# Dilated attention in a two-block model: the value projection with activations stationary

## The chip, the cores and the metric

One core of a Trainium2 chip runs the whole program. The metric is the device time of one execution in microseconds; the kernel is one launch of 2.5 ms, and the change touches one stage of it.

## The reference

The reference is a stack of blocks on a sequence of 256 positions with 1024 features (a first model with memory, RWKV and gated mixers, then a second one with HGRN2 and dilated attention), with feed-forward blocks between. What matters here is the second model's dilated attention:

```python
kv = (_rms(x, kv_norm) @ w_kv).reshape(bsz, seq, 2, B_GROUPS, B_HEADS, B_HEAD_DIM)   # 3 groups, 16 heads of 64
k = _rms(kv[:, :, 0], k_gain[:, None, :])
v = kv[:, :, 1]
...
q = _rms((h @ w_q).reshape(bsz, seq, B_GROUPS, B_HEADS, B_HEAD_DIM), q_gain) * (B_HEAD_DIM ** -0.5)
for g, (window, dil) in enumerate(zip((128, 512, 2048), (1, 4, 16))):
    s = einsum(q_g, k_g) + bias_g          # masked to the band of the window, every dil-th key
    p = exp(s - lse); o_g = p @ v_g
o = sum over g of softmax over g (lse)[g] * o_g
return o.reshape(bsz, seq, 1024) @ w_o
```

Since the three groups are weighted by the softmax of their log-sums, the kernel takes one softmax over the keys of all three.

## The kernel before

**Weights.** Every projection streams its weights as slabs of 128 output features by 1024 inputs (512 KB), through a ring of 4 slots (`raw`, `hi`, `lo`). For each slab s, SyncE loads `raw` once the slot's `lo` is made, ScalarE writes `hi` (`act_hi`, L348, rounded to fp32r) once the slot's old `hi` is used, VectorE writes `lo = raw - hi` (`dve_lo`, L356), and TensorE multiplies. A product in full precision is three fp32r matmuls for each of the 8 blocks of 128 inputs: weights high by activations high (L410), weights high by activations low (L414), weights low by activations high (L415). A slab in `pe_slab` is therefore 24 matmuls, each with a 128x128 piece of the weights stationary and 256 columns (the positions) moving; the result has features on partitions and positions in columns. Engines keep their order by counting semaphores: `lo_ready`, `slab_used`, `banks_freed` (a result bank is evicted), and the stage's own counters `d.<name>`.

**The dilated stage** (class `Dilated`) makes the output in 8 rounds c, each a tile of 128 features, that is two heads in three groups. A round has 9 slabs in a hand-written order: first q, k, v in three groups each (the first round k, q, v), i = 0 to 8. The result banks of the slabs turn through banks 0, 1, 2. Between the slabs TensorE does the attention of this round and the one before; after slab i it does:

- i=1: scores of half 0 of the round before (L1785, 12 small matmuls); i=2: the value transposes (`pe_values`, L1754, 6 transposes by the identity, since the values come out with features on partitions and are wanted with positions there)
- i=2, 3, 4: the query square sums (L1765, 4 matmuls of 2 columns each)
- i=4 and 5: transposes of the probabilities, half 1 (12) and half 0 (6) (L1797)
- i=6: the key square sums (L1739, 6 matmuls), then the output of half 1 (L1812, 24); i=7: the output of half 0 (L1812, 12)
- i=8: the scores of half 1 of this round (L1785)

VectorE evicts each slab's bank times the reciprocal norm (L1960 keys, L1962 queries, L1964 values into `dVF`), makes the low half of the slab four ahead, and does the attention's arithmetic in between: `dve_keys`, `dve_bias` (scores, scales and bias added, L2013, then the largest, L2016, and its negative, L2019), `dve_normalize` (L2026, L2030), `dve_heads` (L2036). ScalarE makes the high half, the squares (L1884), the exponentials (L1921), the copies of the transposed probabilities (L1929) and values (L1912, L1913 into `dVT`) and of the output (L1944).

After the eighth round the output projection's slabs (`so`) are interleaved with what is left of round 7's attention: their first 5 input blocks between the scores, the value transposes and the probability transposes, the rest later.

Of the kernel before, what the change touches and what calls it, by code (L numbers as in the profile page):

```python
# [30 lines left out]
P = 128  # L31
T = 256
# [1562 lines left out]
class Dilated:  # L1595


    FIRST, ORDER = (tuple((x, g) for x in order for g in range(GROUPS)) for order in ("kqv", "qkv"))

    def __init__(self, sh, name, nxt):  # L1600
        self.sh, self.k, self.next_gain = sh, sh.k, nxt
        k, a = sh.k, sh.k.A0
        nc = k.nc
        self.base = sh.stage["dil_k0"].base
        self.so = sh.stage["dil_o"]
        self.K = [k.at(f"dK{z}", a + 3 * z * KB, [P, GROUPS, T]) for z in range(2)]
        self.RK = k.at("dRK", a + 6 * KB, [P, GROUPS, T])
        self.KSQ = k.at("dKSQ", a + 9 * KB, [P, GROUPS, T])
        self.Q = [k.at(f"dQ{z}", a + (12 + 3 * z) * KB, [P, GROUPS, T]) for z in range(2)]
        self.QSQ = k.at("dQSQ", a + 18 * KB, [P, GROUPS, T])  # L1610
        self.VF = k.at("dVF", a + 21 * KB, [P, GROUPS, T])
        self.VT = k.at("dVT", a + 24 * KB, [P, 2, GROUPS, P])
        self.S = k.at("dS", a + 27 * KB, [P, 2, 9, P])
        self.st = k.at("dst", a + 37 * KB, [P, 4, 2, 2])
        self.RQ = k.at("dRQ", a + 37 * KB + 64, [P, 2, 2, GROUPS, 2])
        self.GG = k.at("dGG", a + 37 * KB + 192, [P, GROUPS])
        self.RR = k.at("dRR", a + 38 * KB, [P, T])
        self.B = [k.at(f"dB{z}", (86 + 6 * z) * KB, [P, 2, GROUPS, T]) for z in range(2)]
# [18 lines left out]
    def bank(self, s):  # L1637

        return self.k.bank[(s - self.base) % 3]

# [7 lines left out]
    def turned_banks(self, c, half):  # L1648
# [3 lines left out]
        return ((3, 4), (4, 2)) if c < NC - 1 else ((4, 4), (5, 2))  # L1652

    def value_banks(self, c):

        return 6, 3 if c < NC - 1 else 7

# [12 lines left out]
    def pe(self, pe):  # L1670
# [3 lines left out]
        for c in range(NC):  # L1674
            for i, (x, g) in enumerate(self.order(c)):
                s = self.slab(c, x, g)
                if x == "q":
                    sh.pe_slab(pe, s, self.bank(s), lambda kc: (k.Hh[:, kc, :], k.Hl[:, kc, :]),
                               (lambda kc: pe.wait_ge(k.h_lo, n + kc + 1)) if c == g == 0 else None)
                else:  # L1680
                    sh.pe_slab(pe, s, self.bank(s), lambda kc: (k.Kh[:, kc, :], k.Kl[:, kc, :]),
                               (lambda kc: pe.wait_ge(k.kv_lo, kc + 1)) if c == i == 0 else None)
                if c == 0 and i == 0:
# [4 lines left out]
                if c and i == 1:  # L1688
                    self.pe_scores(pe, c - 1, 0)
                if c and i == 2:  # L1690
                    self.pe_values(pe, c - 1)
                if i == (6 if c else 3):
                    self.pe_key_sums(pe, c)
                if i - (2 if c else 4) in range(GROUPS):
                    self.pe_query_sums(pe, c, i - (2 if c else 4))
                if c and i == 4:
                    self.pe_transposes(pe, c - 1, 1)
                if c and i == 5:
                    self.pe_transposes(pe, c - 1, 0)
                if c and i == 6:  # L1700
                    self.pe_output(pe, c - 1, 1)
                if c and i == 7:
                    self.pe_output(pe, c - 1, 0)
# [6 lines left out]
        early, late = range(last - 2), range(last - 2, last - 1)  # L1710
        sh.pe_slab(pe, s, k.bank[0], moving, ready, chunks=early, whole=False)
        self.pe_scores(pe, last, 0)
        for m in range(1, 3):
            sh.pe_slab(pe, s + m, k.bank[m], moving, chunks=early, whole=False)
        self.pe_values(pe, last)
        sh.pe_slab(pe, s + 3, k.bank[3], moving, chunks=early, whole=False, spare=RING)
# [24 lines left out]

    def pe_values(self, pe, c):

        k = self.k
        k.dve_done.wait(pe, f"d.v{c}")
        k.dve_done.wait(pe, f"d.add{c}.1")
        if c == NC - 1:
            k.dve_done.wait(pe, f"d.ol{c - 1}")
        first, rest = (k.bank[b] for b in self.value_banks(c))
        for half in range(2):  # L1750
            for g in range(GROUPS):
                j = GROUPS * half + g
                out = first[:, j * P:(j + 1) * P] if j < 4 else rest[:, (j - 4) * P:(j - 3) * P]
                ins = pe.transpose(out, self.VF[:, g, half * P:(half + 1) * P], k.ident)  # L1754
        k.pe_done.done(ins, f"d.vt{c}")

# [32 lines left out]
    def pe_transposes(self, pe, c, half):  # L1789

        k = self.k
        k.dve_done.wait(pe, f"d.p{c}.{half}")
        k.act_done.wait(pe, f"d.vt{c}" if half else f"d.pt{c}.1")
        places = [(b, j) for b, n in self.turned_banks(c, half) for j in range(n)]
        per_head = len(places) // 2
        for n, (b, j) in enumerate(places):
            ins = pe.transpose(k.bank[b][:, j * P:(j + 1) * P], self.S[:, n // per_head, 3 * half + n % per_head, :], k.ident)  # L1797
        k.pe_done.done(ins, f"d.t{c}.{half}")

    def pe_output(self, pe, c, half):  # L1800

        k = self.k
        k.act_done.wait(pe, f"d.vt{c}")
        k.act_done.wait(pe, f"d.pt{c}.{half}")
# [11 lines left out]
    def act(self, act):  # L1816
# [4 lines left out]
        for c in range(NC):  # L1821
            for i, (x, g) in enumerate(self.order(c)):
                s = self.slab(c, x, g)
                sh.act_hi(act, s + RING, s % RING, 8, s // RING + 1)
                if c == 0 and i == 1:
# [11 lines left out]
                if c and i == 1:  # L1837
                    self.act_exp(act, c - 1, 1)
                if c and i == 2:
                    self.act_values(act, c - 1)  # L1840
                if i - (1 if c else 3) in range(GROUPS):
# [7 lines left out]
                if i == (4 if c else 6):  # L1849
                    self.act_query_scales(act, c)  # L1850
                if i == (5 if c else 2):
# [6 lines left out]
                if c and i == 7:  # L1858
                    self.act_heads(act, c - 1)
        last = NC - 1  # L1860
        self.act_exp(act, last, 1)
        self.act_values(act, last)
        self.act_exp(act, last, 0)
# [41 lines left out]

    def act_values(self, act, c):

        k = self.k
        k.pe_done.wait(act, f"d.vt{c}")
        first, rest = (k.bank[b] for b in self.value_banks(c))  # L1910
        flat = self.VT[:].rearrange("p h g f -> p (h g f)")
        k.act_done.done(act.activation(flat[:, :512], first[:], ACT.Copy), f"d.vt{c}")  # L1912
        k.act_done.done(act.activation(flat[:, 512:], rest[:, :T], ACT.Copy), f"d.vt{c}")  # L1913

# [31 lines left out]
    def dve(self, dve):  # L1946
# [4 lines left out]
        for c in range(NC):  # L1951
            z = c % 2
            for i, (x, g) in enumerate(self.order(c)):
                s = self.slab(c, x, g)
                if c == 0 and x == "q" and g == 0:
                    k.act_done.wait(dve, "d.rr")
                dve.wait_ge(k.slab_used, s + 1)
                bank = self.bank(s)[:, :T]
                if x == "k":
                    ins = dve.tensor_tensor(self.K[z][:, g, :], bank, k.RKV[:], ALU.mult)  # L1960
                elif x == "q":
                    ins = dve.tensor_tensor(self.Q[z][:, g, :], bank[:, ::-1], self.RR[:], ALU.mult)  # L1962
                else:
                    ins = dve.tensor_tensor(self.VF[:, g, :], bank, k.RKV[:], ALU.mult)  # L1964
                ins.then_inc(k.banks_freed, 1)
                if g == GROUPS - 1:
                    dve.wait_ge(k.banks_freed, RING + s + 1)
                    d(dve.engine_nop(), {"k": f"d.kraw{c}", "q": f"d.qraw{c}", "v": f"d.v{c}"}[x])
                if i == (7 if c else 4):
                    self.dve_keys(dve, c)  # L1970
                sh.dve_lo(dve, s + RING, s % RING, 8)
                if c == 0 and i == 1:
# [5 lines left out]
                if c and i == 3:  # L1978
                    self.dve_normalize(dve, c - 1, 0)
                if c and i == 8:  # L1980
                    self.dve_heads(dve, c - 1)
                if i == 8:
                    self.dve_bias(dve, c, 1)
        last = NC - 1
# [1313 lines left out]
```

## Time and profile before

| | |
|---|---|
| three runs | 2557.51, 2553.10, 2557.44 us, median 2557.44 |
| profiled execution | 2556.5 us, its span 2554.7 us |
| busy in the span | TensorE matmuls 97%, VectorE 68%, ScalarE 52%, GpSimd 3% |
| the dilated stage | about 2060 to 2368 us of the span |

The profile is one execution. Times are from the start of the span. PE is TensorE's matmuls, PEld its loads of the stationary operand, which overlap them; DVE is VectorE, ACT ScalarE. In names such as `bank<-Kh,hi` the moving operand stands first and the stationary one second; `Kh` and `Kl` are the activations for keys and values, `Hh` and `Hl` those for queries. Shapes such as `128*128 128x256` are the stationary and the moving operand.

### The profile page before, as it was taken

The numbers are of one execution on the slowest core, as the hardware profiler recorded it, in microseconds if no ns is written. First come the engines' busy times: TensorE is split into PE (matmuls) and PEld (weight loads), VectorE is DVE, ScalarE is ACT, GpSimd is POOL, SyncE is SP. The second block draws the span as 40 slices with busy tenths as digits, with TensorE's granted clock in tenths as the row PEclk, the third lists the DMA queues.
The fourth block names the chain that finished last, engine by engine and source line by source line (L and its number), as shares of the span: only waits on it lengthen the run. The fifth ranks groups of instructions, "written<-read, shape, count | busy, mean of one in ns | idle before, by whom it ended". The sixth has DMA issues, their size and how long they took to land.

```text
span 2554.7 us, 60487 instructions
## 1 busy us (share of the span) xinstructions
PE 2489.3 (97%) x23329; PEld 2423.8 (95%) x23329; DVE 1744.9 (68%) x2871; ACT 1316.9 (52%) x1997; POOL 79.0 (3%) x122
## 2 busy tenths in 40 slices
PE   8998998999999999999999999899999999999999
PEld 8997977989999999989999999899999999999999
DVE  6757677567766757767766767967667666666774
ACT  5534444455545546555545547455455455555552
POOL 0000442000000000000000000000000000000000
PEclk9999999999999999999999999999999999999999
DMA  6663301435655656445655655246656665553664
GB/s 203 218 211 125 100 12 44 149 126 181 208 185 188 212 202 185 153 136 182 207 181 188 211 176 190 75 126 201 203 173 201 200 188 153 157 157 111 195 210 136
DMA packets 119840, 425.14 MB, mean 166 GB/s; under 512 B 16673, under 2 KB 24564, under 8 KB 119412
## 3 DMA queue, kind: packets, MB, share of 16 engines
q1 hardware_dynamic: 111616, 411.65, 49.7%
q10 hardware_dynamic: 8052, 11.04, 2.3%
q8 instruction: 127, 2.08, 0.3%
q14 instruction: 45, 0.37, 0.0%
HBM read 421.51 MB, written 1.12 MB: 165 GB/s over the span
## 4 chain that ended last, share of the span: by engine, by line
PE 87%; DVE 5%; ACT 3%; issue 2%; POOL 1%; SPq 0%; DMA 0%; ACTq 0%; DVEq 0%; POOLq 0%
PE bank L492 20%; PE bank L487 20%; PE bank L491 20%; PE bank L410 5%; PE bank L415 4%; PE bank L414 4%; ACT hi L348 1%; PE bank L2410 1%; DVE lo L356 1%; PE bank L468 1%; PE bank L470 1%; PE bank L469 1%; PE bank L1812 1%; PE bank L1785 1%; PE bank L1797 1%
## 5 line engine op out<-in xcount | busy, mean ns | idle before, releaser
L356 DVE TENSOR_TENSOR lo<-raw,hi 128x1024 fp32r<-128x1024 f32 (+1 forms) x728 | 935.3, 1293 | 381.0 <-ACT hi L348 379.2
L348 ACT ACTIVATE hi<-raw 128x1024 fp32r<-128x1024 f32 (+1 forms) x728 | 782.2, 1106 | 292.9 <-PE bank L415 168.1
L487 PE MATMUL bank<-Hh,hi 128*128 128x256 f32 x3024 | 836.3, 277 | 3.1 <-DVE lo L356 2.0
L492 PE MATMUL bank<-Hh,lo 128*128 128x256 f32 x3024 | 837.4, 277 | 0.0
L491 PE MATMUL bank<-Hl,hi 128*128 128x256 f32 x3004 | 830.1, 276 | 0.0
L487 PEld LDWEIGHTS bank<-Hh,hi 128*128 128x128 f32 x3024 | 567.9, 188 | 4.3 <-DVE lo L356 4.0
L492 PEld LDWEIGHTS bank<-Hh,lo 128*128 128x128 f32 x3024 | 568.1, 188 | 0.0
L491 PEld LDWEIGHTS bank<-Hl,hi 128*128 128x128 f32 x3004 | 564.3, 188 | 0.0
L487 PE MATMUL bank<-Ah,hi 128*128 128x256 f32 x1408 | 389.7, 277 | 1.9 <-DVE lo L356 1.9
L492 PE MATMUL bank<-Ah,lo 128*128 128x256 f32 x1408 | 390.1, 277 | 0.0
L491 PE MATMUL bank<-Al,hi 128*128 128x256 f32 x1400 | 387.2, 277 | 0.0
L487 PEld LDWEIGHTS bank<-Ah,hi 128*128 128x128 f32 x1408 | 265.1, 188 | 2.1 <-DVE lo L356 2.1
L492 PEld LDWEIGHTS bank<-Ah,lo 128*128 128x128 f32 x1408 | 265.1, 188 | 0.0
L491 PEld LDWEIGHTS bank<-Al,hi 128*128 128x128 f32 x1400 | 263.6, 188 | 0.0
L790 ACT ACTIVATE sgate<-gate 128x256 f32<-128x256 f32 x176 | 73.6, 418 | 228.7 <-DVE gate L823 228.7
L795 ACT ACTIVATE Ah<-act 128x256 f32 (+1 forms) x176 | 73.7, 419 | 215.2 <-DVE act L832 215.2
L410 PE MATMUL bank<-Hh,hi 128*128 128x256 f32 x560 | 160.0, 286 | 0.0
L677 DVE SCALAR_TENSOR_TENSOR X<-bank,X 128x256 f32<-128x256 f32 x112 | 47.5, 424 | 163.0 <-PE bank L492 155.1
L415 PE MATMUL bank<-Hh,lo 128*128 128x256 f32 x560 | 155.9, 278 | 0.0
L414 PE MATMUL bank<-Hl,hi 128*128 128x256 f32 x559 | 155.4, 278 | 0.0
L599 ACT ACTIVATE Hh<-X,vec 128x256 fp32r<-128x256 f32 x96 | 47.8, 504 | 196.6 <-DVE X L677 193.8
L410 PE MATMUL bank<-Kh,hi 128*128 128x256 f32 x384 | 111.6, 291 | 0.0
(445 smaller groups left out, 4042.3 us busy)
## 6 DMA issues: line engine op xcount, KB each, us to landing
raw<-in_w SPq DMA_DIRECT2D x600, 512.0 KB, 3.7
raw<-in_w SPq DMA_DIRECT2D x128, 704.0 KB, 4.9
dB<-dil_bias ACTq DMA_DIRECT2D x16, 384.0 KB, 10.4
X<-in_x SPq DMA_DIRECT2D x2, 512.0 KB, 5.9
mem_x<-in_mem ACTq DMA_DIRECT2D x2, 512.0 KB, 4.4
gWS<-in_ws ACTq DMA_DIRECT2D x1, 1024.0 KB
gBS<-in_bs ACTq DMA_DIRECT2D x1, 1024.0 KB
out_x<-X SPq DMA_DIRECT2D x4, 256.0 KB, 2.6
```

The source lines that it names most:

```text
L348: act.activation(k.hi[:, q, :w], k.raw[:, q, :w], ACT.Copy).then_inc(k.hi_ready, 1)
L356: dve.tensor_tensor(k.lo[:, q, :w], k.raw[:, q, :w], k.hi[:, q, :w].bitcast(F32), ALU.subtract).then_inc(k.lo_ready, 1)
L410: pe.matmul(out, wh, xh, start=first and kc == 0, stop=False)
L414: pe.matmul(out, wh, xl, start=False, stop=False)
L415: mm = pe.matmul(out, wl, xh, start=False, stop=last)
L487: pe.matmul(out, wh, xh, start=first, stop=False)
L491: pe.matmul(out, wh, xl, start=False, stop=False)
L492: mm = pe.matmul(out, wl, xh, start=False, stop=last)
L599: eng.activation(k.Hh[:, c, :], src[:, c, :], ACT.Copy, scale=scale).then_inc(k.h_hi, 1)
L677: dve.scalar_tensor_tensor(k.X[:, c, :], k.bank[s % RING][:, :T], coef, k.X[:, c, :], ALU.mult, ALU.add).then_inc(k.banks_freed, st.per_tile)
L790: act.activation(k.sgate[:, j, :], k.gate[:, j, :], ACT.Silu).then_inc(k.silu_done, 1)
L795: act.activation(k.Ah[:, bass.ds(m, 1), :].rearrange("p a t -> p (a t)"), k.act32[:, j, :], ACT.Copy).then_inc(k.ah_ready, 1)
```

## The change

The value slabs swap roles: a half of the activations (128 positions) is stationary, and the weights move. The result has positions on partitions, as the output matmuls want it. Two of the three value slabs, which lie in neighbouring slots, move side by side in one matmul of 256 columns; the third is done alone in 128 columns. The value transposes and VectorE's value evictions go. ScalarE evicts the value banks with a per-position scale, a column `dRC` that two small matmuls and a copy make once in the first round. The single slab is i=6, the pair i=7 and 8 (group order 2, 0, 1). With the pair come changes of order: output of half 0 moves to i=6, `act_heads` and `dve_heads` come before the splits of i=7, `dve_bias` of half 1 before the low split of i=8, bank numbers skip one a round, and the output projection's first slabs start in another order.

```diff
-    FIRST, ORDER = (tuple((x, g) for x in order for g in range(GROUPS)) for order in ("kqv", "qkv"))
+    FIRST, ORDER = (tuple((x, g) for x in order for g in ((2, 0, 1) if x == "v" else range(GROUPS))) for order in ("kqv", "qkv"))
...
-        return self.k.bank[(s - self.base) % 3]
+        c, i = divmod(s - self.base, 9)
+        return self.k.bank[(8 * c + min(i, 7)) % 3]
+
+    def spare(self, c, i):
+
+        return 4 if c and i < 2 else 3
...
+                elif x == "v":
+                    if i < 8:
+                        self.pe_value_slabs(pe, s, 1 if i == 6 else 2)
...
-                if c and i == 2:
-                    self.pe_values(pe, c - 1)
...
+                if c == 0 and i == 4:
+                    for half in range(2):
+                        ins = pe.matmul(k.bank[7][:, 12 + 2 * half:14 + 2 * half], k.RKV[:, half * P:(half + 1) * P],
+                                        k.ident[:, 0:2], start=True, stop=True)
+                    k.pe_done.done(ins, "d.rc")
...
                 if c and i == 6:
                     self.pe_output(pe, c - 1, 1)
-                if c and i == 7:
                     self.pe_output(pe, c - 1, 0)
...
-        sh.pe_slab(pe, s, k.bank[0], moving, ready, chunks=early, whole=False)
+        sh.pe_slab(pe, s + 1, k.bank[1], moving, ready, chunks=early, whole=False, spare=5)
         self.pe_scores(pe, last, 0)
-        for m in range(1, 3):
-            sh.pe_slab(pe, s + m, k.bank[m], moving, chunks=early, whole=False)
-        self.pe_values(pe, last)
+        sh.pe_slab(pe, s + 2, k.bank[2], moving, chunks=early, whole=False, spare=5)
+        sh.pe_slab(pe, s, k.bank[0], moving, chunks=early, whole=False, spare=1)
+        k.dve_done.wait(pe, f"d.add{last}.1")
...
+    def value_columns(self, w, s, n, kc):
+
+        q, cols = s % RING, slice(kc * P, (kc + 1) * P)
+        if n == 1:
+            return w[:, q, cols]
+        return w[:, q:q + 2, cols] if q < RING - 1 else w[:, ::1 - RING, cols]
+
+    def pe_value_slabs(self, pe, s, n):
+
+        k = self.k
+        pe.wait_ge(k.lo_ready, s + n)
+        pe.wait_ge(k.banks_freed, RING + s - 2)
+        for kc in range(NC):
+            wh, wl = (self.value_columns(w, s, n, kc) for w in (k.hi, k.lo))
+            for half in range(2):
+                out = self.bank(s)[:, half * n * P:(half + 1) * n * P]
+                if n == 2:
+                    out = out.rearrange("p (g f) -> p g f", g=2)
+                xh, xl = (x[:, kc, half * P:(half + 1) * P] for x in (k.Kh, k.Kl))
+                pe.matmul(out, xh, wh, start=kc == half == 0, stop=False, skip_group_check=True)
+                pe.matmul(out, xh, wl, start=False, stop=False, skip_group_check=True)
+                ins = pe.matmul(out, xl, wh, start=False, stop=kc == NC - 1, skip_group_check=True)
+        ins.then_inc(k.slab_used, n)
...
@@ ScalarE
+                if c and i == 7:
+                    self.act_heads(act, c - 1)
+                if i == 7:
+                    self.act_values(act, c, 1)
+                    self.act_values(act, c, 2)
                 sh.act_hi(act, s + RING, s % RING, 8, s // RING + 1)
...
+    def act_values(self, act, c, n):
+
+        k, s = self.k, self.base + 9 * c + 5 + n
+        act.wait_ge(k.slab_used, s + n)
+        act.wait_ge(k.banks_freed, RING + s)
+        if c:
+            k.pe_done.wait(act, f"d.o{c - 1}.0")
+        else:
+            k.act_done.wait(act, "d.rc")
+        for half in range(2):
+            out = self.VT[:, half, 2, :] if n == 1 else self.VT[:, half, :2, :].rearrange("p g f -> p (g f)")
+            ins = act.activation(out, self.bank(s)[:, half * n * P:(half + 1) * n * P], ACT.Copy, scale=self.RC[:, half, 0:1])
+            k.act_done.done(ins, f"d.vt{c}.{n}")
+        k.act_done.wait(act, f"d.vt{c}.{n}")
+        act.sem_inc(k.banks_freed, n)
...
@@ VectorE
-                else:
-                    ins = dve.tensor_tensor(self.VF[:, g, :], bank, k.RKV[:], ALU.mult)
...
                 if i == (7 if c else 4):
                     self.dve_keys(dve, c)
+                if c and i == 7:
+                    self.dve_heads(dve, c - 1)
+                if i == 8:
+                    self.dve_bias(dve, c, 1)
                 sh.dve_lo(dve, s + RING, s % RING, 8)
...
-                if c and i == 8:
-                    self.dve_heads(dve, c - 1)
-                if i == 8:
-                    self.dve_bias(dve, c, 1)
```

## Rows read from the trace of the kernel before

**Rows 1.** The page's busy times, shares of the span and instructions.
```profile
PE 2489.3 (97%) x23329; PEld 2423.8 (95%) x23329; DVE 1744.9 (68%) x2871; ACT 1316.9 (52%) x1997; POOL 79.0 (3%) x122
```
**Rows 2.** TensorE's waits, 2060 to 2365 us: total us, times, longest.
```profile
PE bank L410 <- DVE lo L356: 1.4, 1, 1.4
...
PE bank L1739 <- ACT dKSQ L1853: 0.4, 1, 0.4
```
**Rows 3.** Busy times of one round; columns PE, PEld, DVE, ACT, POOL, PEclk, DMA, GB/s.
```profile
2141.00:2176.60 35.60, 35.60 (x320) 33.88 (x319) 24.70 (x45) 19.85 (x34) 0.00 (x0) 1.00 0.57 156
```
**Rows 4.** TensorE in order of time, second half of a round: start, us, what.
```profile
2144.29 0.37 PE L410 MATMUL bank<-Kh,hi 128*128 128x256 f32 x1
...
2147.12 1.46 PE L1739 MATMUL bank<-dKSQ,masks 128*128 128x256 f32 x6
2148.50 1.53 PE L1812 MATMUL bank<-dPT,dVT 128*64 128x128 f32 x24
2149.96 0.39 PE L410 MATMUL bank<-Kh,hi 128*128 128x256 f32 x1
...
2152.99 0.88 PE L1812 MATMUL bank<-dPT,dVT 128*64 128x128 f32 x12
2153.79 0.38 PE L410 MATMUL bank<-Kh,hi 128*128 128x256 f32 x1
...
2156.81 1.57 PE L1785 MATMUL bank<-dK,dQ 64*128 64x256 f32 x12
2158.31 0.38 PE L410 MATMUL bank<-Hh,hi 128*128 128x256 f32 x1
```
**Rows 5.** TensorE in order of time, at the value transposes.
```profile
2167.68 0.82 PE L1754 MATMUL bank<-masks,dVF 128*128 128x128 f32 x6
2168.34 0.51 PE L1765 MATMUL bank<-sel,dQSQ 128*128 128x2 f32 x4
```
**Rows 6.** Timeline at the first query sum, and at a split slab matmul elsewhere.
```profile
2072.53 0.54 PEld L1765 LDWEIGHTS bank<-sel,dQSQ 128*128 128x128 f32 x4
2072.65 0.50 PE L1765 MATMUL bank<-sel,dQSQ 128*128 128x2 f32 x4
...
2072.98 0.19 PEld L410 LDWEIGHTS bank<-Hh,hi 128*128 128x128 f32 x1
...
46.22 0.30 PEld L396 LDWEIGHTS bank<-Hl,hi 128*128 128x128 f32 x2
46.33 0.30 PE L396 MATMUL bank<-Hl,hi 128*128 128x192 f32 x2
...
46.67 0.28 PE L487 MATMUL bank<-Hh,hi 128*128 128x256 f32 x1
```
**Rows 7.** VectorE in order of time, after a round's end and in the tail.
```profile
2158.07 1.23 DVE L356 TENSOR_TENSOR lo<-raw,hi 128x1024 fp32r<-128x1024 f32 x1 [0.72 <-ACT hi L348]
...
2159.55 2.44 DVE L2013 SCALAR_TENSOR_TENSOR dS<-bank,dRQ,dB 128x256 f32<-128x256 f32 x6
...
2163.88 0.42 DVE L1962 TENSOR_TENSOR dQ<-bank,dRR 128x256 f32<-128x256 f32 x1
...
2171.34 1.15 DVE L2030 TENSOR_SCALAR dS<-dS,dst 128x768 f32<-128x768 f32 x2
...
2344.91 1.15 DVE L2030 TENSOR_SCALAR dS<-dS,dst 128x768 f32<-128x768 f32 x2
```
**Rows 8.** ScalarE in order of time, after a round's end.
```profile
2156.98 1.06 ACT L348 ACTIVATE hi<-raw 128x1024 fp32r<-128x1024 f32 x1 [2.50 <-PE bank L415]
```
**Rows 9.** TensorE in order of time, the wide probabilities' transposes, round and tail.
```profile
2175.16 0.31 PE L1797 MATMUL bank<-masks,dS 128*128 128x128 f32 x1
...
2346.44 0.38 PE L1797 MATMUL bank<-masks,dS 128*128 128x128 f32 x2
```
**Rows 10.** The slab loads (L391) of the stage, from issue to landing.
```profile
DMA to landing us min/median/max: 3.2/4.3/10.8
```

More of the change, by code:

```diff
@@ L1610, in __init__ @@
         self.QSQ = k.at("dQSQ", a + 18 * KB, [P, GROUPS, T])
-        self.VF = k.at("dVF", a + 21 * KB, [P, GROUPS, T])
         self.VT = k.at("dVT", a + 24 * KB, [P, 2, GROUPS, P])
@@ L1617, in __init__ @@
         self.RR = k.at("dRR", a + 38 * KB, [P, T])
+        self.RC = k.at("dRC", a + 39 * KB, [P, 2, 2])
         self.B = [k.at(f"dB{z}", (86 + 6 * z) * KB, [P, 2, GROUPS, T]) for z in range(2)]
@@ L1652, in turned_banks @@
         return ((3, 4), (4, 2)) if c < NC - 1 else ((4, 4), (5, 2))
-    def value_banks(self, c):
-        return 6, 3 if c < NC - 1 else 7
     def block(self, half, e, j):
@@ L1678, in pe @@
                     sh.pe_slab(pe, s, self.bank(s), lambda kc: (k.Hh[:, kc, :], k.Hl[:, kc, :]),
-                               (lambda kc: pe.wait_ge(k.h_lo, n + kc + 1)) if c == g == 0 else None)
+                               (lambda kc: pe.wait_ge(k.h_lo, n + kc + 1)) if c == g == 0 else None, spare=self.spare(c, i))
+                elif x == "v":
+                    if i < 8:
+                        self.pe_value_slabs(pe, s, 1 if i == 6 else 2)
                 else:
                     sh.pe_slab(pe, s, self.bank(s), lambda kc: (k.Kh[:, kc, :], k.Kl[:, kc, :]),
-                               (lambda kc: pe.wait_ge(k.kv_lo, kc + 1)) if c == i == 0 else None)
+                               (lambda kc: pe.wait_ge(k.kv_lo, kc + 1)) if c == i == 0 else None, spare=self.spare(c, i))
                 if c == 0 and i == 0:
@@ L1740, in pe_key_sums @@
         k.pe_done.done(ins, f"d.ks{c}")
-    def pe_values(self, pe, c):
-        k = self.k
[L1745 to L1755, printed above, removed]
+    def value_columns(self, w, s, n, kc):
[4 more added lines that the diff above has]
+    def pe_value_slabs(self, pe, s, n):
+        k = self.k
+        pe.wait_ge(k.lo_ready, s + n)
[11 more added lines that the diff above has]
+        ins.then_inc(k.slab_used, n)
     def pe_query_sums(self, pe, c, g):
@@ L1792, in pe_transposes @@
         k.dve_done.wait(pe, f"d.p{c}.{half}")
-        k.act_done.wait(pe, f"d.vt{c}" if half else f"d.pt{c}.1")
+        if not half:
+            k.act_done.wait(pe, f"d.pt{c}.1")
         places = [(b, j) for b, n in self.turned_banks(c, half) for j in range(n)]
@@ L1802, in pe_output @@
         k = self.k
-        k.act_done.wait(pe, f"d.vt{c}")
+        k.act_done.wait(pe, f"d.vt{c}.2")
         k.act_done.wait(pe, f"d.pt{c}.{half}")
@@ L1838, in act @@
                     self.act_exp(act, c - 1, 1)
-                if c and i == 2:
-                    self.act_values(act, c - 1)
                 if i - (1 if c else 3) in range(GROUPS):
@@ L1850, in act @@
                     self.act_query_scales(act, c)
+                if c == 0 and i == 6:
+                    k.pe_done.wait(act, "d.rc")
+                    d(act.activation(self.RC[:].rearrange("p h n -> p (h n)"), k.bank[7][:, 12:16], ACT.Copy), "d.rc")
                 if i == (5 if c else 2):
@@ L1857, in act @@
                     self.act_key_scales(act, c)
-                if c and i == 7:
-                    self.act_heads(act, c - 1)
         last = NC - 1
         self.act_exp(act, last, 1)
-        self.act_values(act, last)
         self.act_exp(act, last, 0)
@@ L1904, in act_query_scales @@
         k.act_done.done(act.activation(r, r, ACT.Exp, scale=-0.5), f"d.rq{c}")
[L1906 to L1913, printed above, removed]
+    def act_values(self, act, c, n):
[12 more added lines that the diff above has]
+        act.sem_inc(k.banks_freed, n)
     def act_exp(self, act, c, half):
@@ L1956, in dve @@
                     k.act_done.wait(dve, "d.rr")
[L1957 to L1962, printed above, removed]
-                else:
-                    ins = dve.tensor_tensor(self.VF[:, g, :], bank, k.RKV[:], ALU.mult)
[L1965 to L1968, printed above, removed]
+                if x != "v":
+                    dve.wait_ge(k.slab_used, s + 1)
+                    bank = self.bank(s)[:, :T]
+                    if x == "k":
+                        ins = dve.tensor_tensor(self.K[z][:, g, :], bank, k.RKV[:], ALU.mult)
+                    else:
+                        ins = dve.tensor_tensor(self.Q[z][:, g, :], bank[:, ::-1], self.RR[:], ALU.mult)
+                    ins.then_inc(k.banks_freed, 1)
+                    if g == GROUPS - 1:
+                        dve.wait_ge(k.banks_freed, RING + s + 1)
+                        d(dve.engine_nop(), {"k": f"d.kraw{c}", "q": f"d.qraw{c}"}[x])
                 if i == (7 if c else 4):
                     self.dve_keys(dve, c)
+                if c and i == 7:
+                    self.dve_heads(dve, c - 1)
+                if i == 8:
+                    self.dve_bias(dve, c, 1)
                 sh.dve_lo(dve, s + RING, s % RING, 8)
```

## Prediction

> **What bounds the kernel now.** I read four views. The page's first part says who is busiest: TensorE, 2489.3 of 2554.7 us [rows 1]. The waits of TensorE over the whole dilated stage (2060 to 2365 us) come next: four waits, from 1.4 down to 0.4 us, 3.5 us together [rows 2]. Then the busy times of one full round (one output tile c) inside the stage: in 35.6 us TensorE is busy for 35.60, VectorE for 24.70, ScalarE for 19.85, and TensorE's granted clock is 1.00, the 2.4 GHz level [rows 3]. So in this stage a microsecond of TensorE's instruction stream is a microsecond of the kernel, and work taken from VectorE or ScalarE is worth nothing as long as TensorE still finds everything ready. Last, the order of time: TensorE's over the second half of a round [rows 4] and around the value transposes [rows 5], VectorE's [rows 7] and ScalarE's [rows 8], to see how much slack the waits have.
>
> A slab (24 matmuls of 256 columns) runs from 2144.29 to 2147.12, 2.83 us or 118 ns a matmul; after the output matmuls, which leave a short gap, it is 3.03 and 3.02 us [rows 4].
>
> **The slab that stays single.** Weights were stationary: 24 matmuls of 256 columns for each of 3 value slabs, 72 in a round. Now the activations are stationary in halves of 128 positions. The pair of slabs makes 48 matmuls of 256 columns, as many as two slabs had. The third slab, alone, makes 48 matmuls of only 128 columns in place of 24 of 256. The columns are the same, the matmuls and the stationary loads double. This is the term that decides.
>
> What does such a matmul cost? No row has an fp32r matmul of 128 columns, so I bound it. From below: the first of two parts of a split slab matmul, with 192 columns, starts at 46.33 and its neighbours tell the rest: from 46.33 the parts of 192 and 64 columns and the following 256-column matmul take until 46.67, 0.34 us for three [rows 6]. Two whole ones take 0.23, so an extra matmul costs about 0.11 though it adds no column. If columns alone counted, 118 ns for 256 would make 59 for 128. From the other side, the query sums: four matmuls with only 2 moving columns and a 128x128 stationary operand each. Their four loads begin at 2072.53 and the next slab's load at 2072.98: 0.45 us, 112 ns each [rows 6]. Two columns take no time, so 112 ns is what a fresh 128x128 fp32 operand costs by itself, and the split matmul, whose operands are fp32r, agrees. Each of the new 128-column matmuls has its own load too: before the change the page counts as many loads as matmuls, 23329 [rows 1], and the split pair loads the same weights twice [rows 6]. I take 112 ns, between 109, the pace of the six value transposes (0.66 us, [rows 5]), and 118, the slab pace [rows 4]. The Trainium skill ("TensorE: Matmul & The Clock Gate", LDWEIGHTS) puts a load at the number of columns over 1.2 GHz, 107 ns here; the trace's 112 is near it, and by 107 the sum would be 1.9 us lower.
>
> 48 x 0.112 = 5.38 us against 2.83: +2.55 a round, and 8 rounds make **+20.4 us**. (At 109 it is 19.2, at 118 22.7.)
>
> **The pair.** Same matmuls, same columns, the moving operand in two pieces from two ring slots. Nothing interrupts it any more, since the outputs of half 0 go ahead of it. It should take 3.03 for the part after the outputs and 2.83 for the rest, 5.86 against 6.05: -0.19 in the 7 rounds that have outputs, **-1.3**. Zero gain is one bound; the other is 113 ns per matmul, the pace of the slab in [rows 6] (46.22 to 46.33), which makes it -0.4 a round. A moving operand in two far pieces isn't in the trace in this form; a bound from above is the key sums' pace, 1.38 us for 6 matmuls of 256 columns [rows 4], 0.23 each, which would cost some 5.4 us a round. A read address that jumps once in 256 columns is much nearer to a plain one, and I take the slab pace.
>
> **The outputs**, 24 and 12 matmuls, stand together now. The 24 take 1.46 and the 12 take 0.80 (2152.99 to 2153.79) [rows 4]; 12 more cost 0.66, so 36 take 2.12 in place of 2.26: -0.14 x 7 = **-1.0**.
>
> **The value transposes** are gone: 2167.68 to 2168.34, 0.66 us [rows 5]. Seven of the eight sit in the rounds: **-4.6**. The eighth is in the tail below.
>
> **The first round** gains two 2-column matmuls that turn the reciprocal norm to a column: 2 x 0.112 = **+0.2**. VectorE loses 3 evictions of 0.42 [rows 7] a round and ScalarE exchanges two copies for four; both are off TensorE's path, apart from the order of things below.
>
> **The wait that could appear.** The pair gives both slots back at once, so the splits into high and low that were spread over two slabs now come after it. Let P be the end of the pair, where the scores of half 1 start (2156.81 before). Before: the last low split starts at P+1.26 and VectorE starts adding biases at P+2.74; from there to the end of normalizing the wide probabilities (2171.34 plus 1.15, P+15.7) it never pauses [rows 7]. Now ScalarE first evicts the pair, two copies at 0.42 each (the time of VectorE's eviction of as many columns [rows 7]), about P+0.17 to P+1.0, then makes the first high part, 1.06 [rows 8], to P+2.1. VectorE makes the low part to P+3.3, only then adds the biases, and the second low split (1.15 to the next start) has moved behind that. The chain so ends 0.55 + 1.15 = 1.7 us later, at P+17.4 to 17.5. Behind it on TensorE stands the transposing of the wide probabilities. It started at 2175.16 [rows 9], P+18.35; by TensorE's own work it now starts 0.66 earlier, without the value transposes: P+17.7. So there are 0.2 us of slack where there were 2.7. Two other things come late by the same 1.7. The first query bank is evicted after the biases (4.33, 2159.55 to 2163.88) and the second low part (1.15), at P+9.2 [rows 7]; it is wanted when TensorE has done scores (1.50 and some 0.9), three query slabs and a query sum (0.37), at P+11.2, and that is enough. The squares of the last query group stand on ScalarE behind exponentials that wait for VectorE's second maxima, and I find them ready within 0.1 us of when TensorE wants them. I take 0.1 us a round, x 7 = **+0.7**; the bounds are 0 and 0.5 a round (3.5).
>
> The input transfers aren't late: the slot freed by the second low split is now refilled from P+8.9, and its data are wanted by the high part four slabs on, near P+15.9. That leaves 7 us for a landing of 4.3 in the median [rows 10]; the longest took 10.8, and one of these just there would cost some 3 us in one round.
>
> **The tail.** After the last round there are fewer slabs to cover VectorE. Before, the wide probabilities were ready at 2344.91 plus 1.15 = 2346.06 [rows 7] and TensorE took them at 2346.44 [rows 9], with 0.4 us of slack only. VectorE's chain is 1.7 later here too, and the removed value transposes shorten only TensorE's side, which then waits: 1.7 less 0.4, **+1.35** with the handing over (bounds 0 and 2.2).
>
> **The sum.** 20.4 - 1.3 - 1.0 - 4.6 + 0.2 + 0.7 + 1.35 = +15.75 us. The profiled execution took 2556.5 us (span 2554.7 and 1.8 around it), 0.9 under the median of the runs, 2557.44. So 2556.5 + 15.7 = **2572.2 us**, 0.6% slower. Within the mechanism the ends are 2567 (109 ns, 113 in the pair, no waits) and 2579 (118 ns, all waits at their upper bound).
>
> **Rivals.**
> A. The load doesn't bound: a 128-column matmul costs half a 256-column one, 59 ns, the load being hidden under its neighbour. Then the single slab takes 2.83, 20.4 goes out of the sum, and -4.65 is left: 2552, not slower. For it speaks that loads overlap matmuls everywhere; against it the 112 ns of matmuls with 2 columns and the 0.11 us of the split one [rows 6]. It decides below 71 ns a matmul: there the eight slabs cost less than 4.65 us more than before. 3%.
> B. Two matmuls in a row share the stationary xh, and only one of the loads is paid. Then three matmuls cost two loads, 75 ns each, a slab 3.6 us, +6.2 in place of 20.4: 2558, no change. Against it: the split pair, same stationary operand, cost a full 0.11 more [rows 6]. 4%. The Trainium skill (same page, back-to-back issue gap) gives 81 ns per matmul for a stream of loads and matmuls at 128 columns, which would make 2560; the trace's 112 with 2 columns speaks against it here.
> C. VectorE's burst after the pair becomes the bound: the chain ends 1 us later than I added up, and the wide probabilities hold TensorE in each round. Every 1 us of it is 7 us: 2579. For it speaks the slack of 0.2; against it that VectorE has 10 us to spare in a round [rows 3]. 12%.
> D. The two-piece moving operand runs at 0.23 a matmul, the pace of the key sums: 5.4 us a round more, 2615. 1%.
>
> **Chances and range.** Forecast 80%, A 3, B 4, C 12, D 1. The range 2565 to 2580 holds the forecast and nearly all of C. A measurement of this kernel can tell about 0.2% from no change. Faster by over that: a part of A, 2%. Within it: the rest of A, and B, 5%. Slower: 93%.
>
> **What would show it.** Right: round length 35.6 to about 37.2 us; single-slab matmuls 112 ns apart with loads 112 apart; the pair near 5.9; outputs as one block of 36; TensorE's wait for the probabilities at most a few tenths in a round and over 1 us in the tail. Wrong: 128-column matmuls at 60 to 80 ns apart; TensorE idle before the transposes of each round; pair matmuls clearly over 118 ns.

## The result, and the profile after

The changed kernel takes 2571.91 us (median of 5 runs, 2569.68 to 2577.75) against 2557.51 us (median of 5 runs, 2553.1 to 2558.13): ratio 1.0065, 95% interval 1.0054 to 1.0076. It is slower by 0.65%. The profiled execution took 2573.04 us, with a span of 2571.3.

The page's busy times, engine by engine:

```profile
PE 2502.8 (97%) x23477; PEld 2438.7 (95%) x23477; DVE 1733.1 (67%) x2847; ACT 1322.4 (51%) x2014; POOL 78.8 (3%) x122
```

Against [rows 1] VectorE lost 12 us of work and the kernel gained none of it. TensorE's matmuls rose by 148: 8 x 24 more for the single slabs and 4 for the column of norms, less the 48 transposes (6 x 8) that are gone. The code has two matmuls for that column, on fp32 operands; the trace shows four:

```profile
2072.78 0.59 PE L1700 MATMUL bank<-masks,RKV 128*128 128x2 f32 x4
```

To see where the time went, I cut TensorE's order of time at points that both kernels have: the two norm matmuls before the stage, the first score matmul of half 1 in each round (the prediction's P), and the first matmul of the next stage. The pieces in us, and then the blocks of one round:

| | before | after | difference |
|---|---|---|---|
| norm to P of round 0 | 23.57 | 26.46 | +2.9 |
| 7 rounds, P to P | 35.61 each, the first 35.81 | 37.32 each, the first 37.53 | +12.0 |
| last P to the next stage | 33.11 | 34.99 | +1.9 |
| stage | 306.17 | 322.89 | +16.7 |
| single value slab | 2.83 | 5.39 | +2.56 |
| key sums | 1.38 | 1.44 | +0.06 |
| output matmuls | 1.46 and 0.81 | 2.12 | -0.15 |
| the two other value slabs | 3.03 and 3.02 | 5.85 | -0.20 |
| value transposes | 0.66 | none | -0.66 |
| first key slab | 2.82 | 2.91 | +0.09 |

Outside this stage the two kernels are the same program, and so are those of the experiments, yet their profiled executions reach the stage anywhere from 2057.2 to 2065.0 us of the span. Lengths within the stage are the sharper measure, and I go by them.

One full round in the view of windows (columns as in [rows 3]), from P to P:

```profile
2125.66:2162.97 37.31, 37.31 (x337) 35.91 (x336) 23.25 (x41) 20.35 (x36) 0.00 (x0) 1.00 0.56 149
```

TensorE is busy for all of it, as in [rows 3], at a granted clock of 1.00, the 2.4 GHz level. The round is longer by TensorE's own instructions, not by waiting. The timeline shows which. TensorE's matmuls in the single slab:

```profile
2148.18 0.31 PE L1767 MATMUL bank<-hi,Kh 128*128 128x128 f32 x1
2148.32 0.27 PE L1768 MATMUL bank<-lo,Kh 128*128 128x128 f32 x1
2148.43 0.27 PE L1769 MATMUL bank<-hi,Kl 128*128 128x128 f32 x1
2148.55 0.28 PE L1767 MATMUL bank<-hi,Kh 128*128 128x128 f32 x1
...
2153.57 1.51 PE L1745 MATMUL bank<-dKSQ,masks 128*128 128x256 f32 x6
2155.01 2.19 PE L1828 MATMUL bank<-dPT,dVT 128*64 128x128 f32 x36
2157.13 0.39 PE L1767 MATMUL bank<-hi,Kh 128*128 128x256 f32 x1
...
2162.97 1.57 PE L1800 MATMUL bank<-dK,dQ 64*128 64x256 f32 x12
```

and its loads there:

```profile
2148.15 0.19 PEld L1767 LDWEIGHTS bank<-hi,Kh 128*128 128x128 f32 x1
2148.26 0.19 PEld L1768 LDWEIGHTS bank<-lo,Kh 128*128 128x128 f32 x1
2148.37 0.19 PEld L1769 LDWEIGHTS bank<-hi,Kl 128*128 128x128 f32 x1
```

Read the starts, not the durations: a matmul is listed with 0.27 us but they start 0.11 to 0.12 apart, and so do the loads. 48 of them make 5.39 us where the slab of [rows 4] took 2.83. L1767 and L1768 have the same stationary operand, and each has its load all the same. The outputs are one block, 2155.01 to 2157.13, and the pair runs from there to 2162.97, 5.84 us.

TensorE's waits from 2060 to 2385 us (total, times, longest), against [rows 2]:

```profile
PE bank L1800 <- DVE dS L2038: 1.6, 1, 1.6
PE bank L410 <- DVE lo L356: 1.4, 1, 1.4
PE bank L1813 <- DVE dS L2055: 1.3, 1, 1.3
PE bank L1813 <- ACT dPT L1955: 0.7, 1, 0.7
PE bank L1745 <- ACT dKSQ L1875: 0.6, 1, 0.6
```

Each stands once, and all lie in the first round or the tail; none is paid seven times. They are 5.6 us against 3.5. The first was 1.0 before. The new one is the third, the wide probabilities in the tail:

```profile
2362.53 1.53 PE L1813 MATMUL bank<-masks,dS 128*128 128x128 f32 x12 [1.32 <-DVE dS L2055]
```

The chain that the prediction was afraid of, after P = 2162.97. VectorE in order of time, then ScalarE, then TensorE:

```profile
2165.19 1.23 DVE L356 TENSOR_TENSOR lo<-raw,hi 128x1024 fp32r<-128x1024 f32 x1 [6.40 <-ACT hi L348]
2166.33 2.44 DVE L2038 SCALAR_TENSOR_TENSOR dS<-bank,dRQ,dB 128x256 f32<-128x256 f32 x6
...
2179.26 1.15 DVE L2055 TENSOR_SCALAR dS<-dS,dst 128x768 f32<-128x768 f32 x2
```

```profile
2163.08 0.84 ACT L1936 ACTIVATE dVT<-bank,dRC 128x256 f32<-128x256 f32 x2 [4.94 <-PE bank L1769]
2164.09 2.01 ACT L348 ACTIVATE hi<-raw 128x1024 fp32r<-128x1024 f32 x2 [0.17 <-ACT dVT L1936]
...
2179.76 0.40 ACT L1903 ACTIVATE dQSQ<-dQ 128x256 f32<-128x256 f32 x1
```

```profile
2180.39 0.50 PE L1780 MATMUL bank<-sel,dQSQ 128*128 128x2 f32 x4
2180.75 0.41 PE L1813 MATMUL bank<-masks,dS 128*128 128x128 f32 x2
```

The bias begins at P+3.36; the wide probabilities are ready at 2179.26 + 1.15 = 2180.41, P+17.44, and TensorE takes them at 2180.75, P+17.78, after its own work. That leaves 0.34 us. The squares end at 2180.16 and their sum starts at 2180.39: 0.23 us. The chain fits, barely.

### The profile page after: what moved, and what is told of

Same layout as the page of the kernel before. It is cut to its first block, busy times and chain, and to the rows that moved or that the text cites. A ratio compares the mean times of both kernels' runs of the same rounds, so it can differ in the third digit from the quotient of the medians.

```text
span 2571.3 us, 60776 instructions
## 1 busy us (share of the span) xinstructions
PE 2502.8 (97%) x23477; PEld 2438.7 (95%) x23477; DVE 1733.1 (67%) x2847; ACT 1322.4 (51%) x2014; POOL 78.8 (3%) x122
## 4 chain that ended last, share of the span: by engine, by line
PE 85%; DVE 4%; ACT 2%; issue 2%; POOL 1%; ACTq 0%; DMA 0%; DVEq 0%; POOLq 0%
PE bank L492 19%; PE bank L487 19%; PE bank L491 19%; PE bank L410 4%; PE bank L415 3%; PE bank L414 3%; PE bank L2435 1%; PE bank L1767 1%; PE bank L1769 1%; PE bank L1768 1%; PE bank L1331 1%; ACT hi L348 1%; PE bank L468 1%; PE bank L470 1%; PE bank L469 1%
## 5 line engine op out<-in xcount | busy, mean ns | idle before, releaser
L487 PEld LDWEIGHTS bank<-Hh,hi 128*128 128x128 f32 x3024 | 568.3, 188 | 4.6 <-DVE lo L356 4.3
L410 PEld LDWEIGHTS bank<-Hh,hi 128*128 128x128 f32 x560 | 105.8, 189 | 3.9 <-issue 2.5
```

Of the source, the lines that this page charges most:

```text
L410: pe.matmul(out, wh, xh, start=first and kc == 0, stop=False)
L487: pe.matmul(out, wh, xh, start=first, stop=False)
```

## The experiments

In the texts quoted here, a block's length is from its first start to the next block's first start.

### Single slab back to the old roles

Only the term that I held responsible is undone: the single slab has the weights stationary again, VectorE evicts it, two transposes in the next round turn it, and ScalarE copies it. The pair stays swapped.

```diff
-                elif x == "v":
-                    if i < 8:
-                        self.pe_value_slabs(pe, s, 1 if i == 6 else 2)
+                elif x == "v" and i > 6:
+                    if i == 7:
+                        self.pe_value_slabs(pe, s, 2)
...
+                if c and i == 2:
+                    self.pe_single_values(pe, c - 1)
...
+    def pe_single_values(self, pe, c):
+        ...
+        for half in range(2):
+            ins = pe.transpose(k.bank[6][:, half * P:(half + 1) * P], self.VF[:, half * P:(half + 1) * P], k.ident)
```

> The changed kernel with the single value slab turned back: weights stationary, 24 matmuls of 256 columns, one eviction by VectorE, two value transposes and one copy a round; the pair stays swapped. Theory (the stationary loads of the 48 narrow matmuls are the loss): the slab goes from 5.39 to about 2.85 us, two transposes add 0.22, a round from 37.3 to 35.0 us, 8 rounds give back 18.5 us: about 2553.5 us, 0.15% under the kernel before. Rival (the loss comes from the new order and the burst of splits after the pair): the slab's form matters little, the round stays above 36.5 and the time above 2565 us.

Measured: 2553.57 us (median of 11 runs) against 2556.15, ratio 0.9993 (0.9984 to 1.0002). The stage is 304.45 us, 18.4 shorter than the changed kernel's. One round is the distance of these two rows of TensorE's timeline, 35.13 us, with the two value transposes in between (row 2):

```profile
2153.21 0.49 PE L1812 MATMUL bank<-dK,dQ 64*128 64x256 f32 x2
...
2164.28 0.38 PE L1781 MATMUL bank<-masks,dVF 128*128 128x128 f32 x2
2164.50 0.51 PE L1792 MATMUL bank<-sel,dQSQ 128*128 128x2 f32 x4
...
2188.34 0.49 PE L1812 MATMUL bank<-dK,dQ 64*128 64x256 f32 x2
```

The pair, still swapped, takes 5.85 and the single slab 2.91. So the whole loss, and more, sits in the single slab. The swapped pair, whose 48 matmuls keep 256 columns each, costs no more than the 3.03 + 3.02 us that two slabs took before (two slabs in the old roles that stand together take 5.65, as a later experiment shows).

### Half the columns, the same loads

The single slab keeps its 48 matmuls and loads but moves 64 columns in each (the second half of that slab's features is left out). If the columns set the pace the slab halves, if the loads set it nothing changes.

```diff
-            return w[:, q, cols]
+            return w[:, q, kc * P:kc * P + 64]
```

> The changed kernel with 64 moving columns in place of 128 in the single slab's 48 matmuls; the second half of that slab's value features is left out. Theory (the load of the stationary operand sets the pace): matmuls stay 112 ns apart, the slab at 5.4 us, the time within 1 us of the changed kernel, 2572. Rival (columns and a fixed cost set the pace): 64 columns less are 27 ns less, the slab falls to 4.1 us, 8 rounds to about 2561.5 us.

Measured: 2594.78 us, ratio 1.015 (1.0134 to 1.0165), and a stage of 349.72 us. Half of this was as expected. In a stretch at full clock the matmuls with 64 columns start as far apart as those with 128:

```profile
2155.14 0.28 PE L1769 MATMUL bank<-hi,Kh 128*128 128x64 f32 x1
2155.25 0.28 PE L1770 MATMUL bank<-lo,Kh 128*128 128x64 f32 x1
2155.36 0.28 PE L1771 MATMUL bank<-hi,Kl 128*128 128x64 f32 x1
```

So the pace isn't set by the columns, and that rival is refuted. Nor is 112 ns a fixed cost of any matmul with its load. In another stage of the changed kernel, matmuls with 64x64 stationary operands and 32 moving columns start two by two, and the pairs are 58 to 59 ns apart (8 pairs in each line):

```profile
301.05 0.63 PE L2435 MATMUL bank<-rDT,rE 64*64 64x32 f32 x16
301.02 0.55 PEld L2435 LDWEIGHTS bank<-rDT,rE 64*64 64x64 f32 x16
```

What is left is the load of the full 128x128 operand. The total, though, missed its forecast by over 20 us, and the reason is neither theory's. The granted clock (third from the end) over a single slab and over the key sums behind it:

```profile
2111.18:2117.01 5.83, 5.83 (x51) 5.83 (x50) 1.28 (x2) 2.24 (x4) 0.00 (x0) 0.92 0.88 274
2117.01:2119.85 2.84, 2.84 (x7) 1.83 (x8) 1.23 (x1) 1.06 (x1) 0.00 (x0) 0.50 0.25 104
```

and in the changed kernel, with 128 columns, over the slab and over the key sums and outputs behind it:

```profile
2110.86:2116.25 5.39, 5.39 (x51) 5.39 (x50) 1.28 (x2) 2.23 (x4) 0.00 (x0) 1.00 0.94 229
2116.25:2119.81 3.56, 3.56 (x45) 2.96 (x44) 1.27 (x2) 2.95 (x4) 0.00 (x0) 1.00 0.51 203
```

With 64 columns the clock falls in the slab, here near its end, and is at its 1.2 GHz level (0.50) right after. Below it the slab's own matmuls are 213 ns apart and not 112, so that the eight slabs take 5.5 to 7.5 us each. What stands behind the slab pays too, in TensorE's timeline:

```profile
2117.01 2.91 PE L1745 MATMUL bank<-dKSQ,masks 128*128 128x256 f32 x6
2119.85 3.63 PE L1830 MATMUL bank<-dPT,dVT 128*64 128x128 f32 x36
2123.41 0.39 PE L1769 MATMUL bank<-hi,Kh 128*128 128x256 f32 x1
```

The key sums take 2.84 us in place of 1.44 and the outputs 3.56 in place of 2.12, though the profile shows no gap on TensorE.

### Three quarters of the columns

The same with 96 columns (the last quarter is left out), to see whether the pace is still 112 ns and from where on the clock falls.

> The changed kernel with 96 moving columns in the single slab's 48 matmuls; the last quarter of that slab's value features is left out. Theory (loads set the pace): again 112 ns apart, slab 5.4 us as with 64 and with 128 columns. For the clock: with 64 columns the granted clock fell to 0.91 and 0.96 in single rounds and the key sums behind the slab took 2.84 us in place of 1.44. If what TensorE streams in the slab decides, 96 columns should show the same less often or not at all, and the span should be within 3 us of 2571.3; if it is the number of loads, the clock falls as with 64.

Measured: 2590.75 us, stage 343.34, a miss on the total again. In the two slabs through which the clock stayed up, the slab takes 5.38 us, as with 128 columns. The others take 5.8 to 7.1. Two slabs, each with the key sums and outputs that follow it (the granted clock again third from the end):

```profile
2112.61:2117.98 5.37, 5.37 (x51) 5.37 (x49) 1.27 (x2) 2.23 (x4) 0.00 (x0) 1.00 0.94 257
2117.98:2123.18 5.20, 5.20 (x44) 4.03 (x43) 1.70 (x3) 2.95 (x4) 0.00 (x0) 0.67 0.57 209
...
2271.71:2277.09 5.38, 5.38 (x52) 5.38 (x50) 1.28 (x2) 2.23 (x4) 0.00 (x0) 1.00 0.95 271
2277.09:2280.66 3.57, 3.57 (x45) 2.96 (x44) 1.28 (x2) 2.95 (x4) 0.00 (x0) 1.00 0.42 168
```

In the first the clock fell right behind the slab; the second is the only one of the eight where it didn't fall at all, and its round took 37.31 us. So there is one price for 64, 96 and 128 columns at full clock, and the clock falls in both narrower cases, where the changed kernel keeps 1.00. Why it falls isn't shown: both narrower kernels also leave features out, and no run holds the data fixed.

### How much slack the chain has

VectorE gets an extra pass over 768 columns (0.87 us) ahead of the bias, in the changed kernel and in the one before. It uses up slack and gives TensorE no work.

```diff
                 if i == 8:
+                    ...
+                    d(dve.tensor_tensor(self.SCR[:], self.K[z][:], self.K[z][:], ALU.mult), f"d.pass{c}")
                     self.dve_bias(dve, c, 1)
```

> The changed kernel with one more VectorE pass of 768 columns (about 0.85 us, into a scratch area) ahead of the biases of half 1 in every round. Theory (VectorE's chain after the pair has only 0.34 us of slack: probabilities ready at P+17.44, taken at P+17.78): TensorE now waits 0.5 us before the wide probabilities' transposes in each round, the round goes from 37.3 to 37.8, and the tail gains 0.85: span about 4.5 us over the changed kernel's 2571.3. Rival (VectorE has 10 us to spare in a round, so nothing happens): span unchanged but for the tail.

> The same VectorE pass in the kernel before. Theory (there the slack was 2.7 us): the rounds stay at 35.6 us, TensorE waits only in the tail, where 0.4 us of slack leave about 0.5 us: span 2555.2. Rival (any VectorE work at that place costs its time): span 2561.

Measured: in the changed kernel (2577.84 us) each round grows by 0.71 us, to 38.03, and the tail by 1.06. In the kernel before (2558.9 us) the rounds stay at 35.61 and the tail grows by 0.87. TensorE's waits in the changed kernel with the pass:

```profile
PE bank L1801 <- DVE dS L2043: 2.5, 1, 2.5
PE bank L1781 <- ACT dQSQ L1904: 2.4, 7, 0.4
```

and the place in a round where the second stands:

```profile
2181.58 0.61 PE L1781 MATMUL bank<-sel,dQSQ 128*128 128x2 f32 x4 [0.30 <-ACT dQSQ L1904]
```

Cut into blocks, the 0.71 is 0.46 of waiting for the squares, 0.11 in the query sum behind it, 0.20 because two slabs run at 118 and not 113 ns a matmul, and -0.06 elsewhere. The pass puts VectorE 0.87 us back (2166.83 to the next start at 2167.70); TensorE itself comes 0.23 later to the sum and waits 0.46, so the changed kernel had 0.87 - 0.23 - 0.46 = 0.18 us of slack there, near the 0.23 in the order of time above. What binds first is the query squares (seven times), not the probabilities. For the probabilities the kernel before had 2.7 us of slack, and the changed one has 0.34. The kernel before pays nothing for the same pass in its rounds. In its tail it pays more than the 0.45 that the slack of 0.4 would leave, since its wait for the wide scores is on TensorE's path as well:

```profile
PE bank L1786 <- DVE dS L2018: 1.8, 1, 1.8
```

1.8 us where it was 1.0.

### The outputs together, in the kernel before

One line moves the outputs of half 0 to i=6, as the change does, with no role swapped.

```diff
                     self.pe_output(pe, c - 1, 1)
-                if c and i == 7:
                     self.pe_output(pe, c - 1, 0)
```

> The kernel before with one line moved: the output of half 0 right behind that of half 1. Theory: 36 matmuls in one block cost 2.12 us, the break costs 0.14, a round goes from 35.61 to 35.47 us and nothing else moves: 1.0 us in all. Rival (the probabilities of half 0 aren't copied yet, TensorE waits): the round grows.

> The kernel before with the two outputs together, timed (the single look gave rounds of 35.07 us in place of 35.61, and a stage 3.8 us shorter). Theory: 3.8 us under the kernel before, 0.15%: ratio 0.9985, about as fast as or faster than the mixed kernel (0.9993). Rival (the stage's gain is lost elsewhere in the program): ratio 1.000.

Measured: a round of 35.07 us, 0.54 shorter, where 0.14 was forecast. The second and third value slab, now one after the other:

```profile
2188.33 0.39 PE L410 MATMUL bank<-Kh,hi 128*128 128x256 f32 x1
...
2189.13 0.28 PE L410 MATMUL bank<-Kh,hi 128*128 128x256 f32 x1
...
2189.47 0.28 PE L410 MATMUL bank<-Kh,hi 128*128 128x256 f32 x1
...
2193.98 0.49 PE L1784 MATMUL bank<-dK,dQ 64*128 64x256 f32 x2
```

5.65 us in place of 3.03 + 3.02, which is 0.40 less; the outputs give 0.14. Each time output matmuls and a slab meet, some 0.1 us goes at either side (here 2193.98 less the last matmul's start at 2193.78, 0.20 where the pace is 0.11), and there is one such pair of joints less: 0.2. The other 0.2 is the pace: three matmuls from 2189.13 to 2189.47, 113 ns each, where the two slabs of [rows 4] run at 118. Timed, with 12 runs: 2552.53 against 2553.67, ratio 0.9991 (0.9979 to 1.0003), a gain that the stage's 302.35 us shows and the total can't yet tell from none.

### The change's order alone

The change's order inside the rounds, none of its roles: outputs together, heads before the splits of i=7, bias before the low split of i=8. The group order of the values, the bank numbers and the start of the output projection stay as they were.

```diff
-                if c and i == 7:
                     self.pe_output(pe, c - 1, 0)
...
+                if c and i == 7:
+                    self.act_heads(act, c - 1)
                 sh.act_hi(act, s + RING, s % RING, 8, s // RING + 1)
...
+                if c and i == 7:
+                    self.dve_heads(dve, c - 1)
+                if i == 8:
+                    self.dve_bias(dve, c, 1)
                 sh.dve_lo(dve, s + RING, s % RING, 8)
```

> The changed kernel's order without the swapped roles: all three value slabs with weights stationary and the six value transposes, the outputs together, the heads ahead of the splits of slab 7, the biases of half 1 ahead of the low split of slab 8. Theory (the loss is the narrow matmuls alone, and the new order by itself is a gain through the joined outputs): rounds 35.07 us, the tail 33.0 to 33.2, all of it about 2553.5 us, 4 us under the kernel before. Rival (the moved work of VectorE costs something by itself): rounds over 35.3 or a tail over 34 us.

Measured: 2550.18 us against 2553.67, ratio 0.9986 (0.9977 to 0.9995); rounds of 35.07, a tail of 32.92, a stage of 302.17 us, 4.0 less than before. Its stage is the shortest of the study, and it is the only version faster than the kernel before whose interval excludes no change; in time it can't be told from the one with the outputs together (0.9991). In the tail the wait for the wide scores (1.0 before) is gone, and one of 0.5 us for the wide probabilities has come.

The stage gives the split of the whole change: the order inside the rounds is worth -4.0 us (-3.8 of it from the outputs together), and all the rest, the swapped roles with the new start of the output projection, +20.7 on top of it.

### The first experiment's kernel with a tail of its own

The single slab in the old roles and the pair swapped, and in the last round the bias goes before the low splits on VectorE and the output projection's slabs cover the chain.

```diff
-                sh.dve_lo(dve, s + RING, s % RING, 8)
+                if c < NC - 1 or i < 7:
+                    sh.dve_lo(dve, s + RING, s % RING, 8)
+                if c == NC - 1 and i == 8:
+                    sh.dve_lo(dve, s - 1 + RING, (s - 1) % RING, 8)
...
+        sh.dve_lo(dve, self.so.base + 3, (self.so.base + 3) % RING, 8)
```

> The mixed kernel (single slab as before, pair swapped) with another order in the last round: VectorE adds the biases ahead of both low splits and makes the second only after the wide probabilities; the output projection's slab 0 goes ahead of slab 2, and slab 3 comes after the first transposes. Theory: the tail is held by VectorE's late start after the pair (TensorE's waits of 1.5 and 1.0 us); the outputs of the last round end about 1.6 us earlier counted from the pair's end, at P+17.5 and not P+19.2: about 2552 us, 0.2% under the kernel before. Rival (waits only move, since VectorE's work is the same): the tail as long as it was.

Measured: a tail of 33.13 us, 1.46 shorter than the 34.59 of the first experiment's kernel, and a stage of 302.99. In time 2553.09 against 2555.23, ratio 0.9993 (0.9981 to 1.0005): no difference that can be told, and the 0.2% that was forecast isn't shown. The tail's cost was an order that could be mended, but the swapped pair then still gains nothing over the order alone (302.17).

## Why the prediction was right

2572.2 us was forecast and 2571.91 measured. That the two are 0.3 us apart is luck: the five runs lie from 2569.68 to 2577.75, and the change is +14.4 by the medians and +16.5 by the profiled executions. What was right is the mechanism, and that is seen in the stage (+15.75 forecast, +16.7 measured), term by term:

- **The single slab** (+20.4): seven times 2.56 in the rounds and 2.48 in the first (5.39 against 2.91), 20.4. The pace, 111 to 112 ns with 128 columns, is that of the matmuls with 2 columns in [rows 6], and 64 and 96 columns have it too at full clock. Rival A (59 ns) and rival B (one load for two matmuls) are both out: each matmul has its load, and the loads are 111 ns apart. The Trainium skill ("TensorE: Matmul & The Clock Gate", back-to-back issue gap) gives about 81 ns for such a stream; the trace has 112 here, and the measurement decides.
- **Pair and outputs** (-1.3 and -1.0): 5.85 and 2.12, or -0.20 and -0.15 a round, as forecast. The gain comes from the outputs standing together, not from the swap: the old roles with the same order take 5.65, at 113 ns a matmul, and the swapped pair stays at the 118 that I had taken, so that the order alone is worth 0.54 a round where the change has 0.35. Rival D (230 ns) is out.
- **The value transposes** (-4.6): 0.66 a round gone, as forecast.
- **The first round**: +2.9 in place of 2.55 + 0.2; no outputs stand in it, so the pair gains nothing there. The column of norms takes 0.45 and not 0.2: it is four matmuls in the trace where the sum had the two of the code.
- **Waits in the rounds** (+0.7): none, so this term was wrong, and other things filled its place. The squares were ready 0.2 us early, the probabilities 0.3. In their place stand two things that I didn't book, 0.06 in the key sums and 0.09 in the first key slab: a round is +1.71 where the sum had 1.65 with the wait and 1.55 without. Rival C is out for this kernel, but close: with 0.87 us more on VectorE a round grows by 0.71, of which 0.57 is this chain. There the squares bound, which I had named as the other thing that comes late.
- **The tail** (+1.35): the wait came, 1.3 us before the wide probabilities, and their transposes are at P+12.96 where they were at P+11.56, +1.40. (The wait for the scores before them grew as well, from 1.0 to 1.6 us, but those 0.6 us lie inside the 1.40.) Another 0.4 us comes from the output projection's slabs, whose matmuls run at 118 ns and not 113, and makes +1.9.

The upper end of the forecast, 2579, comes to 2578.2 by its own terms (22.7 - 1.3 - 1.0 - 4.6 + 0.2 + 3.5 + 2.2 on 2556.5); nothing hangs on it.

Left open: slabs of 256 columns run at one of two paces, 113 or 118 ns a matmul, each held over many matmuls. Of the distances between neighbouring matmuls of slabs with 256 columns, the stage before had 880 of 112 to 115 ns and 836 of 116 to 120; the changed kernel has 553 and 1016. What selects the pace I haven't settled. It carries 0.2 us of each pair, the 0.09 of the first key slab and the tail's 0.4, not the result.

Open too is what makes the load of a full operand take 112 ns. The 64x64 operands above show a smaller one at 58 to 59, but no run varied the operand's size in the value slab itself.

## What to carry to other kernels

Count loads, not only columns, before you swap operands: here a matmul with a fresh 128x128 stationary operand costs 112 ns at full clock with 2, 64, 96 or 128 moving columns, and 113 to 118 with 256, so cutting a 256-column matmul in two nearly doubles its cost. Work taken from an engine that has time to spare gains nothing: here VectorE's evictions. The transposes that TensorE was spared (0.66 us a round) were small against the 2.56 that it was given. A rearrangement that comes bundled with a change should be timed without it: here the order was the good half.

## What the runs showed that I had not expected

- The granted clock fell where the profile shows no gap on TensorE. In the rounds shown, with 64 columns, each matmul with its load, its mean was 0.92 over the slab and 0.50 over the key sums behind it; with 96 columns it was 1.00 and then 0.67; with 128 columns it stayed at 1.00. The slab and what follows it pay: stages of 349.7 and 343.3 us against 322.9, with fewer columns to move.
- A matmul on fp32 operands in the code can be two in the trace: the column of norms is two calls and four matmuls, 0.45 us. Count them in the trace before you price them.
- A slab of 256 columns has two paces, 113 and 118 ns a matmul, and edits that don't touch it move it from one to the other: the extra VectorE pass took two slabs from 5.65 to 5.85 us, moving the outputs took two from the 118 pace to the 113.
